# Decoder chain on one core: the state-space drive moved three units earlier, its four output products to units 66 to 69, and narrower waits ahead of the output product

## What is computed

```python
proj = rmsnorm(x, norm_mix_pre) @ w_in            # q, k, v of attention | u_ssm | q_mem
y_na  = neighbourhood_attention(q, k, v, rpb)
y_ssm = s5_mixer(u_ssm, ...)                      # forward and reverse state-space scan, then gelu and a gate
y_mem = memory_cross_attention(q_mem, mem, ...)
y = concat(rmsnorm(y_na), rmsnorm(y_ssm), rmsnorm(y_mem))
x = x + rmsnorm(y @ w_out, norm_mix_post)

# inside s5_mixer, per direction: bu = u * b_bar ; h[t] = lam_bar * h[t-1] + bu[t] ; y = c * h (real part)
# y = gelu(y_f + y_b + d * u) ; y = y * sigmoid(y @ w_glu + b_glu)
```

## Time and profile before

| what | value |
|---|---|
| median of 3 runs | 3538.91 us (3538.85 to 3539.88) |
| profiled execution, its own time | 3540.97 us |
| its span, first to last instruction | 3539.1 us |
| mean granted clock of TensorE | 0.989 of 2.4 GHz |
| busy: PE / PEld / DVE / ACT / POOL | 3446.3 / 2815.7 / 1951.7 / 1619.9 / 285.7 us |
| share of the chain that ended last: PE / POOL / DVE / ACT | 92 / 3 / 3 / 1 % |

### The profile page before, as it was taken

How to read it: one execution, slowest core, us unless ns; L and a number is a source line. 1 busy time by engine, 2 the same in 40 slices (tenths; PEclk the granted TensorE clock), 3 DMA queues, 4 the chain that set the end, 5 groups by cost and what they waited for, 6 DMA issues and landing times.

```text
span 3539.1 us, 42654 instructions
## 1 busy us (share of the span) xinstructions
PE 3446.3 (97%) x15818; PEld 2815.7 (80%) x15818; DVE 1951.7 (55%) x2300; ACT 1619.9 (46%) x2068; POOL 285.7 (8%) x402
## 2 busy tenths in 40 slices
PE   8999999999999999999999999999989999999998
PEld 7788878888888787777878878888878778888886
DVE  4544475555555755566675545566534745555555
ACT  4544444444444355454444444455545644444443
POOL 0000000000000000002480003000460000000000
PEclk9999999999999999999999999999999999999999
DMA  7555566566556565456556547656544455556553
GB/s 230 167 170 175 178 186 189 180 192 194 183 187 198 156 185 153 128 177 175 184 176 198 188 154 228 198 178 184 167 143 140 152 175 187 188 189 189 189 188 122
DMA packets 335043, 630.09 MB, mean 178 GB/s; under 512 B 33228, under 2 KB 35504, under 8 KB 333376
## 3 DMA queue, kind: packets, MB, share of 16 engines
q1 hardware_dynamic: 330416, 611.59, 55.6%
q0 software_dynamic: 4496, 16.73, 1.6%
HBM read 624.86 MB, written 2.33 MB: 177 GB/s over the span
## 4 chain that ended last, share of the span: by engine, by line
PE 92%; POOL 3%; DVE 3%; ACT 1%; issue 1%; DMA 0%; SPq 0%; ACTq 0%; DVEq 0%
PE psum L257 28%; PE psum L259 27%; PE psum L258 27%; PE psum L311 3%; PE psum L471 1%; PE psum L473 1%; PE psum L472 1%; POOL big L1100 1%; POOL scratch L1102 1%; POOL scratch L1101 1%; DVE weights_lo L219 1%; PE psum L741 0%; ACT weights_hi L212 0%; PE psum L2683 0%; DVE x L1760 0%
## 5 line engine op out<-in xcount | busy, mean ns | idle before, releaser
L219 DVE TENSOR_TENSOR weights_lo<-weights_raw,weights_hi 128x1024 fp32r<-128x1024 f32 x1155 | 1429.1, 1250 | 1219.3 <-ACT weights_hi L212 1218.2
L212 ACT CAST weights_hi<-weights_raw 128x1024 fp32r<-128x1024 f32 x1155 | 1210.1, 1050 | 1710.1 <-PE psum L259 1688.6
L257 PE MATMUL psum<-weights_hi,act_hi 128*128 128x512 f32 x3112 | 1238.6, 398 | 10.2 <-DVE weights_lo L219 5.8
L259 PE MATMUL psum<-weights_hi,act_lo 128*128 128x512 f32 x3112 | 1216.2, 391 | 0.0
L258 PE MATMUL psum<-weights_lo,act_hi 128*128 128x512 f32 x3112 | 1214.4, 390 | 0.0
L257 PEld LDWEIGHTS psum<-weights_hi,act_hi 128*128 128x128 f32 x3112 | 586.0, 188 | 135.6 <-issue 16.4
L259 PEld LDWEIGHTS psum<-weights_hi,act_lo 128*128 128x128 f32 x3112 | 585.2, 188 | 125.5
L258 PEld LDWEIGHTS psum<-weights_lo,act_hi 128*128 128x128 f32 x3112 | 586.5, 188 | 115.5
L257 PE MATMUL psum<-weights_hi,hid_hi 128*128 128x512 f32 x1336 | 530.4, 397 | 3.3 <-DVE weights_lo L219 2.0
L259 PE MATMUL psum<-weights_hi,hid_lo 128*128 128x512 f32 x1336 | 520.8, 390 | 0.0
L258 PE MATMUL psum<-weights_lo,hid_hi 128*128 128x512 f32 x1336 | 520.6, 390 | 0.0
(11 more groups left out here) (389 smaller groups left out, 1750.5 us busy)
## 6 DMA issues: line engine op xcount, KB each, us to landing
weights_raw<-in_ffn_wgu SPq DMA_DIRECT2D x352, 512.0 KB, 4.3
weights_raw<-in_w_ff SPq DMA_DIRECT2D x256, 512.0 KB, 3.9
weights_raw<-in_ffn_wd SPq DMA_DIRECT2D x176, 512.0 KB, 3.8
weights_raw<-in_even_w_in SPq DMA_DIRECT2D x120, 512.0 KB, 3.6
weights_raw<-in_odd_w_in SPq DMA_DIRECT2D x64, 512.0 KB, 3.7
weights_raw<-in_w_in SPq DMA_DIRECT2D x64, 512.0 KB, 3.6
weights_raw<-in_odd_w_o SPq DMA_DIRECT2D x32, 512.0 KB, 3.8
weights_raw<-in_w_out SPq DMA_DIRECT2D x32, 512.0 KB, 3.8
```

The costliest lines, as they stand in the source:

```text
L212: nc.scalar.copy(w_hi[:, u % SPLIT_SLOTS, :size], raw[:, u % RAW_SLOTS, :size]).then_inc(hi_ready, 1)
L219: nc.vector.tensor_tensor(w_lo[:, u % SPLIT_SLOTS, :size], raw[:, u % RAW_SLOTS, :size], w_hi[:, u % SPLIT_SLOTS, :size].bitcast(F32), ALU ...
L257: nc.tensor.matmul(o, ah, wh, start=(k + j == 0), stop=False)
L259: last = nc.tensor.matmul(o, al, wh, start=False, stop=(k + j == kts - 1))
```

## The change

- **The drive earlier.** The eight DMAs of u are issued after load 17 in place of 20, the transpositions come beside units 12 and 13 in place of 15 and 16, the drive beside 16 to 23 in place of 19 to 26. Two transpositions of queries (units 17 and 18) now fall into the drive; ACT takes them ahead of the drive's copies.
- **The turning back later.** ACT waits for `ssm_h` at e = 61 in place of 58 and turns back at 61 to 64, with the tile `bias` as spare room.
- **The outputs later.** The four groups stand beside units 66, 67, 68 and 69. The gelu moves from e = 73 to 75, its two transpositions from units 75 and 76 to 77 and 78.
- **Narrower waits.** Each of the five runs of the output product waits for the two turns that filled its own part of `aT`, in place of both banks free.

```diff
@@ SP, beside_loads
-                if u == 20:
+                if u == 17:
                     sp.wait_ge(ready("ssm_u"), 1)
@@ second_act
-            if e in (15, 16):
-                if e == 15:
+            if e in (12, 13):
+                if e == 12:
                     act.wait_ge(ready("ssm_u4_clear"), 1)
...
-            if 19 <= e < 27:
-                j, ri = (e - 19) // 2, (e - 19) % 2
+            for at_e, to in ((17, qT[0]), (27, kT[0]), (41, qT[1]), (49, kT[1]), (65, qT[2])):
+                if e in (at_e, at_e + 1):
+                    k = 2 * (e - at_e)
+                    act_turn(act, c, to[:, k:k + 2, :].rearrange("p k t -> p (k t)"))
+            if 16 <= e < 24:
+                j, ri = (e - 16) // 2, (e - 16) % 2
+                t = c.n["turn"]
                 act.wait_ge(turned, c.now("turn", 1))
...
-            if 58 <= e < 62:
-                if e == 58:
+            if 61 <= e < 65:
+                if e == 61:
                     act.wait_ge(ready("ssm_h"), 1)
-                q = e - 58
+                q = e - 61
...
-                kept = kT[0][64:128, 2 * (q % 2):2 * (q % 2) + 2, :].rearrange("p a (n e) -> p (a n) e", e=64)
+                kept = bias[64:128, 2 * (q % 2):2 * (q % 2) + 2, :].rearrange("p a (n e) -> p (a n) e", e=64)
...
-            if e in (62, 63, 64, 69):
-                b = (62, 63, 64, 69).index(e)
+            if 66 <= e < 70:
+                b = e - 66
                 act.wait_ge(turned, c.now("turn", 1))
...
-            if e == 73:
+            if e == 75:
                 act.wait_ge(ready("ssm_yin"), 16 * TT * T4)
                 A_(y_ssm[:], y_ssm[:], ACT.Gelu_apprx_tanh).then_inc(ready("ssm_gelu"), 1)
@@ second_pe (second_dve has the same numbers)
-            if v in (15, 16):
-                if v == 15:
+            if v in (12, 13):
+                if v == 12:
                     pe.wait_ge(ready("ssm_ux"), 16 * TT * T4)
...
-            if 19 <= v < 27:
-                if v == 19:
+            if 16 <= v < 24:
+                if v == 16:
                     all_turned()
...
                 if v in (at_v, at_v + 1):
                     pe.wait_ge(att_done, n)
+                    out_turns.append(c.n["turn"])
...
-            if v in (62, 63, 64, 69):
-                b, t = (62, 63, 64, 69).index(v), next_turn()
+            if 66 <= v < 70:
+                b, t = v - 66, next_turn()
                 if b == 0:
                     pe.wait_ge(ready("ssm_turned_back"), 4)
...
-            for at_v, s_, k0 in ((75, "ssm_gelu", 0), (85, "ssm_out", 0)):
+            for at_v, s_, k0 in ((77, "ssm_gelu", 0), (85, "ssm_out", 0)):
@@ the output product
             for k0, n in ((0, 4), (4, 4), (12, 1), (8, 4), (0, 4)):
-                all_turned()
+                for _ in range(2):
+                    turn_stands(pe, out_turns.pop(0))
```

More of the change, by code:

```diff
@@ L1455, in second_act @@
                 done("ssm_u")
-            if e in (15, 16):
-                if e == 15:
+            if e in (12, 13):
+                if e == 12:
                     act.wait_ge(ready("ssm_u4_clear"), 1)
                 act.wait_ge(turned, c.now("turn", 1))
-                nc.scalar.copy(u4x[0:64, 8 * (e - 15):8 * (e - 15) + 8, 0, :],
+                nc.scalar.copy(u4x[0:64, 8 * (e - 12):8 * (e - 12) + 8, 0, :],
                                psum[0:64, 4 + t % 2, :].rearrange("p (j n) -> p j n", j=8)).then_inc(turn_hi, 1)
@@ L1478, in second_act @@
                 c.n["split_turn"] += 1
[L1479 to L1482, removed]
             i = sec_starts(e - 1)
@@ L1512, in second_act @@
                 act.wait_ge(att_done, (32, 40, 48)[g])
+                if e == 66:
+                    act.wait_ge(ready("ssm_turned_back"), 4)
                 for m in range(TT):
@@ L1521, in second_act @@
                 evac_at(act, c, e, b0, lambda m, o: nc.scalar.copy(acc[(e - 65) // 2][:, m, :], o))
-            if e == 73:
+            if e == 75:
                 act.wait_ge(ready("ssm_yin"), 16 * TT * T4)
                 A_(y_ssm[:], y_ssm[:], ACT.Gelu_apprx_tanh).then_inc(ready("ssm_gelu"), 1)
-            if e in (75, 76):
-                k = 12 + 2 * (e - 75)
+            if e in (77, 78):
+                k = 12 + 2 * (e - 77)
                 turn_take_hi(act, c, aT_hi[:, k:k + 2, :].rearrange("p k t -> p (k t)"))
@@ L2131, in second_dve @@
                 gained_lo(dve, c, 2 * (e + 8), g_mix[:, 2 * (e + 8):2 * (e + 8) + 2])
-            if e in (15, 16):
+            if e in (12, 13):
                 t = c.n["turn"]
-                if e == 15:
+                if e == 12:
                     dve.wait_ge(ready("ssm_u4_clear"), 1)
                 dve.wait_ge(turn_hi, c.now("split_turn", 1))
-                V.tensor_copy(u4x[64:128, 8 * (e - 15):8 * (e - 15) + 8, 1, :],
+                V.tensor_copy(u4x[64:128, 8 * (e - 12):8 * (e - 12) + 8, 1, :],
                               psum[64:128, 4 + t % 2, :].rearrange("p (j n) -> p j n", j=8)).then_inc(turn_free[t % 2], 1)
@@ L2149, in second_dve @@
                 c.n["split_turn"] += 1
-                if e == 26:
+                if e == 23:
                     done("ssm_driven")
@@ L2500, in even_pe @@
                 turn(pe, c, [dqT[:, h + j, m * P:(m + 1) * P] for j in range(2) for m in range(TT)])
-        lead_turns, latent_turns = [], []
+        lead_turns, latent_turns, out_turns = [], [], []
         def odd_pe(v):
@@ L2638, in second_pe @@
                 for n in range(8):
-                    j = 8 * (v - 15) + n
+                    j = 8 * (v - 12) + n
                     of = ux[:, 2 * j:2 * j + 2, :, :].rearrange("p g s e -> p (g s e)")
@@ L2648, in second_pe @@
                     turn(pe, c, [tok_rows[:, m, (h + j) * P:(h + j + 1) * P] for j in range(2) for m in range(TT)])
-            if 19 <= v < 27:
-                if v == 19:
+            if 16 <= v < 24:
+                if v == 16:
                     all_turned()
-                j, ri, b = (v - 19) // 2, (v - 19) % 2, next_turn()
+                j, ri, b = (v - 16) // 2, (v - 16) % 2, next_turn()
                 for n in range(4):
```

## The result

The changed kernel takes **3518.48 us** (median of 6 runs, 3517.16 to 3519.97), against 3540.14 (3538.85 to 3541.71, 6 runs) for the kernel before, run beside it. The ratio is 0.9939 with a 95% interval of 0.9929 to 0.9948: faster by 21.7 us. The forecast was 3517.8.

What follows compares the result with a forecast made beforehand. PE's matmul stream was taken to bound the kernel, so only its idle time counts: 13.26 (stop) + 2.80 (slow restart) + 5.01 (short stops) = 21.07 us, taking 3538.91 to 3517.8 us, range 3515.6 to 3523.0.

Steps and rivals of the forecast that it cites:

- What bounds: Third block's mixer: PE is 92% of the chain, so an edit is worth only the PE idle time it removes.
- The scan's length: POOL's scan: 82.7 us of free steps plus 34.6 us for 36 splits, running from 2512.7 to 2630.2.
- the price of a split: POOL's scan beside DVE: each split running beside it costs the scan 0.96 us.
- The rival with the whole split's length: POOL's scan: each split costs 1.24 us, scan ends 2641.5, PE stops 6.3 us, total 3526.9; chance 3%.
- The late wait: ACT's wait for `ssm_h`: asked at 2632.9, 2.7 us after the scan's end, so PE's 13.26 us stop goes.
- The stop and its restart: PE after unit 59: the 13.26 us stop and 2.80 us of slow restart both go.
- The margin on PE's side: PE near unit 61: feels a late scan only from 2635.2, through the exponential at e = 62; margin 5 us.
- ACT at e = 61 to 64: ACT's turning back: about 1 us behind at e = 63, given back at e = 64; cost 0, otherwise 1 to 2 us.
- The narrower waits and the short stops: PE's five short stops of 0.49, 0.67, 0.85, 0.16 and 2.84 us all go: 5.01 us, bounds 0 and 5.0.
- The early DMAs and the drive at 16 to 23: DMAs of u land by 2466.7 to 2467.7, PE asks at 2468.7; cost 0, up to 2 us if landing slips.
- Queries and drive share each unit: Units 17 and 18: banks asked for again after one unit; taken as 0, at most a 2.84 us wait.
- The number: Whole kernel: 21.07 us saved from the median of 3538.91 us gives 3517.8 us; forecast's chance 69%.

Runs made afterwards that it cites:

- e3: Changed kernel with the drive, its transpositions and the DMAs of u back at their old units: 3521.96 us, ratio 0.9948 to the kernel before.
- e4: Changed kernel with the turning back at e = 58 to 61 and outputs beside 62, 63, 64 and 69 again: 3529.31 us, ratio 0.9969 to before.
- e6: Changed kernel with 20 more POOL instructions between the scan's end and its flag: 3528.41 us, ratio 0.9967 to the kernel before.
- e5: Changed kernel with 5 more POOL instructions between the scan's end and its flag: 3518.42 us, ratio 0.9936 to the kernel before.
- e9: Changed kernel with the wide wait (both banks free) required again ahead of unit 64 only: 3520.09 us, ratio 0.9946 to the kernel before.
- e2: Kernel before the change with the narrower waits alone added: 3534.66 us, ratio 0.9984 to the kernel before.
- e7: Changed kernel with the gelu at e = 73 and its transpositions at 75 and 76 again: 3517.89 us, ratio 0.9935 to the kernel before.
- e1: Changed kernel with the wide waits (both banks free) back ahead of all five output runs: 3526.14 us, ratio 0.9961 to the kernel before.
- e8: Changed kernel with the wide wait (both banks free) required again ahead of unit 80 only: 3522.31 us, ratio 0.9950 to the kernel before.

## Why the prediction was right, step by step

- **What bounds.** PE's idle time in this mixer was the whole effect: 22.22 us gained there, PE without a wait, and 21.7 us by the timed runs.
- **The scan's length.** Start, end and the price of a split came out within 0.3 us and 0.01 us. The same rule fits four scans: 113.4 us with 32 splits before, 117.8 with 37 after, 115.9 and 115.8 with 35 in e3 and e4: 0.96, 0.95, 0.95 and 0.95 us. (36 splits were forecast in the sum; the rival had 37.) The rival with the whole split's length, 1.24 us for each, is out, and the trace shows why. One place of after, DVE and POOL:

```profile
2539.85 1.23 DVE L219 TENSOR_TENSOR weights_lo<-weights_raw,weights_hi 128x1024 fp32r<-128x1024 f32 x1 [1.63 <-ACT weights_hi L212]
```

```profile
2540.01 1.25 POOL L1101 TENSOR_TENSOR scratch<-scratch,big 128x64 f32<-128x64 f32 x1
```

 It is the same at all 32 splits before and all 37 after. An instruction of POOL that already runs when the split starts ends in its usual time (0.32 or 0.46 us). Exactly one starts within the split; it runs 1.18 to 1.53 us and ends 0.18 to 0.32 us behind the split. So POOL is held every time, but not for the whole 1.24 us: the held instruction starts on average 0.16 us into the split, and what is left of it behind the split is about 0.14 us shorter than a free one: 1.25 - 0.16 - 0.14 = 0.95. The Trainium skill, page "SBUF — State Buffer", section "SBUF: two separate sides", has the loser of the shared ports block for the other's whole instruction, and the trace agrees: nothing of POOL that started within a split ended before it.
- **The late wait.** ACT asked at 2633.1 in the time of before (forecast 2632.9) and ACT's margin was 2.6 us (forecast 2.7). The stop and its restart were 16.06 us by forecast; up to the score product of unit 60, 2643.40 before and 2628.07 after, they gave 15.33 + 0.89 = 16.22.
- **Where I was wrong inside a right answer.** The margin on PE's side was said to be 5 us, the exponential at e = 62 being the first thing PE needs from behind the wait. For that path it was right: e3 and e6 (the flag's time less the stop for L767) put the point from which PE stands for the exponential at 2634.9 in the time of before (forecast 2635.2). But PE feels the scan sooner, by way of DVE's split and L791: with ACT 1.10 us late in e5, PE stood 0.65 us and the mixer grew by 1.02. So the true margin was ACT's own 2.6 us and hardly more. It cost nothing here, as ACT didn't wait.
- **ACT at e = 61 to 64.** Falling behind by about 1 us at e = 63 was right; it was not given back at 64 but by the split of e = 67, and PE, with split units in hand, did not stop. What the moved steps meant for unit 64 wasn't seen: with the old wait there, and no output group beside unit 63 to fill the time, the change would have cost 2.38 us more (e9). Only the narrow wait made the term 0.
- **The narrower waits and the short stops.** Here is the mis-sized term: 5.01 us by the forecast, 22.22 - 16.22 = 6.00 by the trace. I summed idle times. The three stops that e2 takes out were worth 4.98 us for 4.36 of idle; that of 0.16 us was worth 0.12 (e7 against after); the 0.9 us that are left go with the stop of 0.49 us and the outputs that were reordered around it, and no run splits them further. With the 0.16 us by which the stop of 13.26 and its restart exceeded 16.06, this is the difference between 21.1 and 22.2.
- **The early DMAs and the drive at 16 to 23.** No wait came with them. The eight DMAs (durations, first and last start, then landing) are, to be read with the earlier trace rows:

```profile
L977 SPq DMA_DIRECT2D scratch<-big x8: 662/672/1519, 2458.5 to 2464.4; - x8
...
DMA to landing us min/median/max: 2.8/3.1/3.8
```

 The last lands by 2468.2, and PE's transposition follows at 2469.61 without waiting. Queries and drive share each unit without one too:

```profile
2485.79 0.60 PE L311 MATMUL psum<-ident,big 128*128 128x128 f32 x4
2486.22 1.06 PE L2657 MATMUL psum<-big,big 128*128 128x128 f32 x8
2489.89 0.60 PE L311 MATMUL psum<-ident,big 128*128 128x128 f32 x4
2490.33 1.06 PE L2657 MATMUL psum<-big,big 128*128 128x128 f32 x8
```

- **The number.** The mixer gained 1.15 us more than forecast, and the kernel came out 0.7 us above it: it was 0.9 us late already ahead of the mixer, and the median of before in these runs was 3540.14 in place of 3538.91. Neither has to do with the change, and both lie within the scatter of 1 to 3 us between runs. A result within 0.7 us of the forecast is in part luck: a gain under-read by 1.15 us in the trace and a base 1.2 us too low stand against each other.

## What to carry to other kernels

A stop of the bounding engine that the profile puts down to a small copy may be made one engine further back: look at what the copy's own engine waited for just ahead of it, and move that wait behind the work that others need. A wait for everything outstanding is cheap until something else in the schedule slips, so narrow it to what the next product reads before moving steps around it (e1: the wide waits cost 4.98 us in the old schedule and 8.15 in the new). And when a long chain of small instructions runs on POOL beside DVE, price it per instruction of DVE that falls beside it: here, starting it 7 us earlier made it 4.4 us longer.

## What the runs showed that I had not expected

- **The same idle time, two clocks.** Behind an idle of 2.84 us PE ran on at full clock in the kernel before (1.00), and behind 2.84 and 2.85 us ahead of the same unit its clock was 0.50, the 1.2 GHz level (2721.00 to 2724.41 in e1, 2716.21 to 2719.63 in e8 with matmuls 0.43 us apart). What PE did ahead of it is nearly the same list of instructions, but not quite. Counted back from the matmul behind the stop, the last stop lies 13 us back in the kernel before (0.16 us), over 30 us in e1 and over 60 in e8, and the two transpositions of the gelu's result lie 10.3 and 6.7 us back in e1 and e8, 17.5 and 13.3 in the kernel before. I have no run that tells what decides it (the wide wait at unit 80 with the gelu at its old place was not run); the price of such a stop is 2.84 us in one case and 4.4 in the other, so it belongs in the range, not in the sum.
- **A short stop costs more than its row.** Three stops in e2 cost 0.62 us beyond the idle recorded, at full clock, and the three in e3 (2.27 us, 2.75 in the mixer) 0.48. In e2 most of it is how the row is made: the matmuls of 512 columns start 0.23 us apart, but each is listed with 0.39 or 0.40 us, so the idle is counted from an end that lies 0.16 us behind the point where the next would have started.
- **A restart at half clock is not all or nothing.** Behind 13.26 us the piece of the program from the heads' transposition to the next score product took 6.01 us (clock 0.50), behind the 8.32 us of e4 4.81 (2631.47 to 2636.28), against 3.21 undisturbed. In e4 the clock was at 0.50 for 3.41 us of it and back at 1.00 for the rest:

```profile
2631.47:2634.88 3.41, 3.41 (x10) 2.87 (x11) 1.91 (x5) 3.30 (x8) 0.00 (x0) 0.50 0.30 83
2634.88:2636.28 1.40, 1.40 (x7) 1.12 (x6) 0.87 (x2) 0.03 (x1) 0.00 (x0) 1.00 0.46 171
```
